# Attention scores of a two-layer step as three rounded products, with smaller buffers around them

## What is computed

```python
def _sink_attend(q, k, v, mask, sink):
    s = jnp.einsum('bqhgd,bkhd->bhgqk', q.astype(jnp.float32), k.astype(jnp.float32)) * (HEAD_DIM ** -0.5)
    if mask is not None:
        s = jnp.where(mask, s, -jnp.inf)
    sk = sink.astype(jnp.float32).reshape(1, N_KV_HEADS, GROUP, 1)
    m = jnp.maximum(jnp.max(s, axis=-1), sk)
    p = jnp.exp(s - m[..., None])
    den = jnp.sum(p, axis=-1) + jnp.exp(sk - m)
    o = jnp.einsum('bhgqk,bkhd->bqhgd', p, v.astype(jnp.float32))
    return (o / jnp.transpose(den, (0, 3, 1, 2))[..., None]).astype(q.dtype)
# latent: q = _axial_rope(q); k = _axial_rope(k); keys = [256 cached, 384 around the block of 128 queries]
# 16 heads of 64, 4 of them to each of 4 key/value heads; out = x + gate * (o * silu(g)) @ w_out
```

## Time and profile before

| | us |
|---|---|
| median of 3 runs | 2796.76 (2796.53 to 2798.9) |
| the profiled execution | 2798.01 |
| its span in the profile | 2796.2 |
| first stage (norms, loads) | about 0 to 110 |
| attention of 4 key/value heads | about 110 to 1109 |
| attention output | about 1123 to 1385 |
| mLSTM, 8 heads | about 1390 to 2590 |
| last output | to the end |

### The profile page before, as it was taken

The page is one execution under the profiler, slowest core; times in us unless marked ns, Lnnn a source line. Parts: engine busy times, 40 slices in busy tenths (PEclk is TensorE's granted clock), DMA queues, the critical chain, the costliest instruction groups (busy, mean ns, idle before and its releaser), DMA issues.

```text
span 2796.2 us, 46819 instructions
## 1 busy us (share of the span) xinstructions
PE 2690.0 (96%) x16995; PEld 2311.2 (83%) x16995; DVE 1259.6 (45%) x3434; ACT 822.2 (29%) x2140; POOL 639.2 (23%) x792
## 2 busy tenths in 40 slices
PE   6899999999999998899999999999999999998898
PEld 3687787878778786688699999899999999998787
DVE  3645637464664647555224242423334241514533
ACT  3433515242442425122213122222213131312111
POOL 2511030112113010433103031221213040303432
PEclk9999999999999999899999999999999999999999
DMA  9511030102102011344103131222222030316343
GB/s 352 204 54 55 2 96 2 54 28 69 40 17 73 24 41 68 130 136 136 41 21 82 41 69 46 60 62 36 86 36 79 18 105 16 82 41 191 109 143 106
DMA packets 183958, 213.29 MB, mean 76 GB/s; under 512 B 26288, under 2 KB 131712, under 8 KB 181840
## 3 DMA queue, kind: packets, MB, share of 16 engines
q1 hardware_dynamic: 173776, 183.18, 22.8%
q10 hardware_dynamic: 9984, 27.37, 2.5%
HBM read 172.44 MB, written 38.07 MB: 75 GB/s over the span
## 4 chain that ended last, share of the span: by engine, by line
PE 56%; DVE 2%; DMA 1%; issue 1%; POOL 0%; SPq 0%; ACT 0%; DVEq 0%; POOLq 0%
PE psum L522 11%; PE psum L524 11%; PE psum L523 11%; PE psum L1284 2%; PE psum L1285 2%; PE psum L1286 2%; PE psum L2145 2%; PE psum L1703 2%; PE psum L1705 2%; PE psum L1704 2%; PE psum L2209 2%; PE psum L2212 2%; PE psum L2193 1%; DMA m_bc<-gate_rows_mlstm 1%; PE psum L2136 1%
## 5 line engine op out<-in xcount | busy, mean ns | idle before, releaser
L522 PE MATMUL psum<-h_hi,m_w_lo 128*128 128x384 f32 (+1 forms) x1600 | 605.0, 378 | 4.7 <-DVE m_w_lo L507 3.6
L524 PE MATMUL psum<-h_hi,m_w_hi 128*128 128x384 f32 (+1 forms) x1600 | 574.4, 359 | 0.0
L523 PE MATMUL psum<-h_lo,m_w_hi 128*128 128x384 f32 (+1 forms) x1600 | 573.9, 359 | 0.0
L522 PEld LDWEIGHTS psum<-h_hi,m_w_lo 128*128 128x128 f32 x1600 | 302.0, 189 | 27.8 <-issue 5.2
L524 PEld LDWEIGHTS psum<-h_hi,m_w_hi 128*128 128x128 f32 x1600 | 301.0, 188 | 27.2
L523 PEld LDWEIGHTS psum<-h_lo,m_w_hi 128*128 128x128 f32 x1600 | 302.5, 189 | 20.4
L522 PE MATMUL psum<-h_hi,attn_w_lo 128*128 128x384 f32 (+1 forms) x800 | 291.1, 364 | 1.2 <-DVE attn_w_lo L507 0.9
L524 PE MATMUL psum<-h_hi,attn_w_hi 128*128 128x384 f32 (+1 forms) x800 | 285.8, 357 | 0.0
L523 PE MATMUL psum<-h_lo,attn_w_hi 128*128 128x384 f32 (+1 forms) x800 | 285.3, 357 | 0.0
L790 ACT ACTIVATE arena<-arena,negm 128x640 f32<-128x640 f32 (+2 forms) x208 | 161.8, 778 | 188.3 <-DVE negm L852 188.3
L491 POOL CAST m_w_hi<-m_w_raw 128x512 fp32r<-128x512 f32 x80 | 49.8, 623 | 714.5 <-PE psum L524 651.2
(11 more groups left out here) (275 smaller groups left out, 4820.1 us busy)
## 6 DMA issues: line engine op xcount, KB each, us to landing
m_bc<-gate_rows_mlstm SPq DMA_DIRECT2D x128, 256.0 KB, 3.7
m_w_raw<-in_mlstm_w_in SPq DMA_DIRECT2D x40, 512.0 KB, 4.8
h_full<-gated_output SPq DMA_DIRECT2D x31, 512.0 KB, 4.1
gated_output<-gT SPq DMA_DIRECT2D x8, 1088.0 KB, 5.1
layer_output<-xb_out ACTq DMA_DIRECT2D x17, 512.0 KB, 2.6
h_hi_full<-layer_output SPq DMA_DIRECT2D x17, 512.0 KB, 4.7
out<-h_hi_full ACTq DMA_DIRECT2D x17, 512.0 KB, 4.9
xb<-in_x_sample ACTq DMA_DIRECT2D x16, 512.0 KB, 6.4
```

The lines of the kernel that those rows point to most:

```text
L522: pe.matmul(out, self.lo[:, k, :], E.h_hi[:, k, tok], start=(k == 0), stop=False)
L523: pe.matmul(out, self.hi[:, k, :], E.h_lo[:, k, tok], start=False, stop=False)
L524: ins = pe.matmul(out, self.hi[:, k, :], E.h_hi[:, k, tok], start=False, stop=(k == KT - 1))
```

## The change

- The scores become three products of rounded parts: q_lo k_hi, q_hi k_lo, q_hi k_hi; the context block stays f32. ACT rounds keys group by group (k_hi, with the cached keys as a sixth part) and queries in four parts (q_hi); DVE makes k_lo and q_lo, which lie in the memory of kT and qT themselves. k_lo of the first two groups is made behind m=0's g=3 and g=4, of the other three behind m=1's g=0 to 2, and that of the cached keys, with q_lo, before the gate's first unit.
- ACT rounds m=1's weights before g=3 of the keys, where it did so first.
- One shuffle buffer in place of two: a shuffle waits for POOL's last addition. q_hi lies over the buffers of cosine and sine, so their first loads for m=0 and m=3 also wait until the scores are done.
- `sarg` is gone: the sink's exponential is exp(negm + sink) with the sink as bias, one instruction for each head.
- The weights' difference in a pass is made by halves, at s = 6 and s = 8.
- `wmask` has 5 blocks; block 0 reads it as two slices, side by side in a strided view. The small statistics share a buffer, and the key/value output lies in probT.
- The attention output's weights come 5 of 8 slices ahead in place of 6, by two loads.
- In the mLSTM steps the second slice `ahead(2s+1)` comes before the products of the values.

```diff
+        split = lambda name, at0, cols: nc.alloc_sbuf_tensor_at(name, [P, cols], F32R, offset=at0)
+        k_lo = split("k_lo", sb.at, KREQ)
         kT = sb("kT", [P, KCOLS])
         gT = sb("gT", [P, T])
         vS = sb("vS", [P, VTILES, HD])
+        q_lo = split("q_lo", sb.at, SAMPLE)
         qT = sb("qT", [P, T])
         spare = E.arena
+        q_hi = split("q_hi", E.arena_at + 3 * 4 * D, SAMPLE)
...
-        shuf = [spare[:, 5, b * 512:(b + 1) * 512] for b in range(2)]
-        pair = spare[:, 6:8, :].rearrange("p a n -> p (a n)")
-        prob = [pair[:, b * 640:(b + 1) * 640] for b in range(3)] + [sb("prob3", [P, 640])[:, :]]
+        shuf = spare[:, 5, 0:512]
+        flat = spare[:, :, :].rearrange("p a n -> p (a n)")
+        prob = [flat[:, 5 * D + 512 + b * 640:5 * D + 512 + (b + 1) * 640] for b in range(4)]
...
+                    if g == 0 and m != 1:
+                        sp.wait_ge(s_S, at(kv * (2 * NU) + (NU if m == 3 else 0)))
...
-                        n_ahead = E.w_ahead
-                        sp.dma_start(spare[:, 0:n_ahead, :], E.a["attn_w_out"][0].rearrange("(k p) m -> p k m", p=P)[:, 0:n_ahead, :]).then_inc(s_wo, 16)
+                        w_out = E.a["attn_w_out"][0].rearrange("(k p) m -> p k m", p=P)
+                        sp.dma_start(spare[:, 0:3, :], w_out[:, 0:3, :]).then_inc(s_wo, 16)
+                        sp.wait_ge(s_S, at(NKV * (2 * NU)))
+                        sp.dma_start(spare[:, 3:E.w_ahead, :], w_out[:, 3:E.w_ahead, :]).then_inc(s_wo, 16)
...
-                    J.act_hi(act, kv * 5 + 1, kv * 6 + 3)
                     for g in range(NG):
+                        if g == 3:
+                            J.act_hi(act, kv * 5 + 1, kv * 6 + 3)
...
+                        act.wait_ge(s_kdup, at(kv * NG + g + 1))
+                        act.copy(k_hi[:, keys_part(g)], kT[:, keys_part(g)]).then_inc(s_khi, 1)
...
-                            act.wait_ge(s_sarg, at(bbase + b + 1))
-                            act.activation(esink[:, b % 2, :], sarg[:, b % 2, :], ACT.Exp).then_inc(s_es, 1)
+                            for hh in range(2):
+                                col = kv * 4 + 2 * sub + hh
+                                ins = act.activation(esink[:, b % 2, hh:hh + 1], negm[:, b % 2, hh:hh + 1], ACT.Exp,
+                                                     bias=sink[:, col:col + 1])
+                            ins.then_inc(s_es, 1)
...
+                        act.wait_ge(s_rope, at(kv * ROPES + NG * (2 + sub)))
+                        for i in range(QPARTS):
+                            act.copy(q_hi[:, queries_part(i)], qT[:, queries_part(i)]).then_inc(s_qhi, 1)
...
-                    dve.wait_ge(s_rope, at(kv * ROPES + (rope - 1 if rope >= 2 else 0)))
+                    dve.wait_ge(s_rope, at(kv * ROPES + rope))
                     settle(E, dve)
-                    dve.stream_shuffle(shuf[b][0:rows, 0:wl], bank[0:rows, 0:wl], SWAP).then_inc(s_shuf, 1)
+                    dve.stream_shuffle(shuf[0:rows, 0:wl], bank[0:rows, 0:wl], SWAP).then_inc(s_shuf, 1)
...
-                            if hh == 1:
-                                dve.wait_ge(s_nm, at(base + w + 1))
-                                dve.wait_ge(s_es, at(bbase + (b - 1 if b >= 2 else 0)))
-                                dve.tensor_tensor(sarg[:, b % 2, :], negm[:, b % 2, :],
-                                                  sink[:, ds(kv * 4 + 2 * sub, 2)], ALU.add).then_inc(s_sarg, 1)
...
+                        def keys_low(i):
+                            c = keys_part(i)
+                            dve.wait_ge(s_khi, at(kv * (NG + 1) + i + 1))
+                            dve.tensor_tensor(k_lo[:, c], kT[:, c], k_hi[:, c], ALU.subtract).then_inc(s_klo, 1)
+
+                        def queries_low(i):
+                            c = queries_part(i)
+                            dve.wait_ge(s_qhi, at((kv * 2 + sub) * QPARTS + i + 1))
+                            dve.tensor_tensor(q_lo[:, c], qT[:, c], q_hi[:, c], ALU.subtract).then_inc(s_qlo, 1)
...
+                                if g >= 3:
+                                    keys_low(g - 3)
...
+                                if m == 1 and g < 3:
+                                    keys_low(NG - 3 + g)
                             else:
+                                if g == 0:
+                                    if m == 2:
+                                        keys_low(NG)
+                                    for i in range(QPARTS):
+                                        queries_low(i)
...
-                            if s == 6 and not (last and m == 4):
-                                J.dve_lo(dve, kv * 5 + m + 1)
+                            if s in (6, 8) and not (last and m == 4):
+                                J.dve_lo(dve, kv * 5 + m + 1, (s // 2 - 3,))
...
-                        for hh, r in enumerate(rows):
-                            pe.matmul(E.bank[2 * hh][:, 256:512], q[hh], kT[r, 0:PAST], start=True, stop=True)
-                        for hh, r in enumerate(rows):
-                            pe.matmul(E.bank[2 * hh + 1][:, 0:k1 - k0], q[hh], kT[r, k0:k1],
-                                      start=True, stop=True).then_inc(s_S, 1)
+                        t = slice(b * P, (b + 1) * P)
+                        parts = ((q_lo, k_hi), (q_hi, k_lo), (q_hi, k_hi))
+                        for n, (x, y) in enumerate(parts):
+                            for hh, r in enumerate(rows):
+                                pe.matmul(E.bank[2 * hh][:, 256:512], x[r, t], y[r, 0:PAST], start=(n == 0), stop=(n == 2))
+                        for n, (x, y) in enumerate(parts):
+                            for hh, r in enumerate(rows):
+                                ins = pe.matmul(E.bank[2 * hh + 1][:, 0:k1 - k0], x[r, t], y[r, k0:k1],
+                                                start=(n == 0), stop=(n == 2))
+                                if n == 2:
+                                    ins.then_inc(s_S, 1)
...
-                    pe.wait_ge(s_rope, at(kv * ROPES + NG * (2 + sub)))
+                    pe.wait_ge(s_qlo, at((kv * 2 + sub) * QPARTS + QPARTS))
                     pe.wait_ge(s_release, at(kv * NB + NG * m))
                     if sub == 0:
                         pe.wait_ge(s_kdup, at(kv * NG + NG))
-                        pe.wait_ge(s_ckl, at(kv * 16 + 16))
+                        pe.wait_ge(s_klo, at(kv * (NG + 1) + NG + 1))
...
+                        ahead(2 * s + 1)
...
-                        ahead(2 * s + 1)
...
-    window = np.concatenate([own, own, prev, own, nxt] + [own, own, own, nxt], 1)
+    window = np.concatenate([own, own, prev, own, nxt], 1)
```

More of the change, by code:

```diff
@@ L570, in phase_attn @@
         s_wo = sem("w_out_loaded")
+        s_khi, s_klo, s_qhi, s_qlo = (sem(x) for x in ("keys_hi", "keys_lo", "queries_hi", "queries_lo"))
         (s_shuf, s_cos, s_rope, s_gth, s_release, s_kdup, s_vT, s_vS, s_kvo, s_kvst, s_ckl, s_cvl,
@@ L608, in scores_of, with window, keys_part @@
             return pair[:, first:first + width(w // 2)]
+        def window(b):
+            if b == 0:
+                return bass.AP(tensor=E.wmask[:, :].tensor, offset=0, ap=[[MASK, P], [3 * P, 2], [1, 2 * P]])
+            return E.wmask[:, 0:width(b)]
+        def keys_part(i):
+            if i == NG:
+                return slice(0, PAST)
+            t0, wl, wc = lat_ctx(i)
+            return slice(KLAT + t0, KLAT + t0 + wl)
+        queries_part = lambda i: slice(i * 512, i * 512 + 512)
+        QPARTS = SAMPLE // 512
         weighted, spread = E.bank[6][:, 0:P], E.bank[6][:, P:2 * P]
@@ L763, in _ @@
                     act.copy(kvout[:, 1, :], E.bank[6][:, 0:HD]).then_inc(s_kvo, 1)
+                    act.wait_ge(s_ckl, at(kv * 16 + 16))
+                    act.copy(k_hi[:, keys_part(NG)], kT[:, keys_part(NG)]).then_inc(s_khi, 1)
                     for sub in range(2):
@@ L844, in softmax_max @@
                             n = width(b)
-                            m0 = WFIRST if b == 0 else WMID
                             dve.wait_ge(s_S, at(base + w + 1))
@@ L849, in softmax_max @@
                             dve.wait_ge(s_p, at(base + (2 * b - 2 if b >= 2 else 0)))
-                            dve.wait_ge(s_sarg, at(bbase + (b - 1 if b >= 2 else 0)))
+                            dve.wait_ge(s_es, at(bbase + (b - 1 if b >= 2 else 0)))
                             settle(E, dve)
-                            dve.tensor_tensor_reduce(prob[w % 4][:, 0:n], scores_of(w), E.wmask[:, m0:m0 + n],
+                            x, y = prob[w % 4][:, 0:n], scores_of(w)
+                            if b == 0:
+                                x, y = (t.rearrange("p (a n) -> p a n", a=2) for t in (x, y))
+                            dve.tensor_tensor_reduce(x, y, window(b),
                                                      scale=-(HD ** -0.5), scalar=nsk[:, 2 * sub + hh:2 * sub + hh + 1],
```

(4 more changed lines are left out.)

37 lines of the change are left out of this document (18 added, 19 removed).

## The result

The changed kernel takes **2812.1 us** (median of 5, 2810.31 to 2814.23) beside 2796.76 us (2795.03 to 2800.23) before: 15.3 us more, a ratio of 1.0052, interval 1.0038 to 1.0067. The forecast was 2791, with a range that ended at 2801. It is slower by more than the 0.2% that can be told from no change, the outcome that had been given 0.12. The profiled execution has a span of 2812.4 us and a mean granted clock of 0.985.

The account below looks back on a forecast made before the run. Two equal attention bounds, PE's work and the DVE/ACT chain. Passes -9.6, key heads +9.6, mLSTM -4.8 and loads -0.7 sum to -5.5 us: 2792.5 on the profiled 2798.0, 2791.3 against the median; forecast 2791, range 2780 to 2801.

Parts of the forecast that it names:

- What bounds the kernel: Attention steps: PE's own work, 3.88 us a step, and the chain through DVE and ACT, 3.875, bind equally.
- The score parts: Attention scores: three rounded products shorten a block's score time S by 0.19 us; blocks 0 and 1 give -0.33 a pass.
- exposed loads: Rival in the attention scores: weight loads of each part are not hidden, +28 us, 2829 in all; 7%.
- unpaired heads: Rival in the attention scores: heads' pairs not side by side in rounded form, parts three times as long, near 2870; 3%.
- the sink's exponential: Attention chain on ACT: a second instruction ahead of the copies adds 0.094 us, leaving 3.825 us a step.
- -9.6 us for the passes: Attention, eight passes: shorter scores less the second sink exponential give -1.2 us a pass, 0 to -15 in all.
- The key head: Start of the three key heads after the first: rotary rounds in series and the keys' difference add 3.2 us each, +9.6.
- The clock: Rival at the key heads: the 3.2 us stalls make the granted clock fall, +5 us, 2796; 10%.
- ACT's cast: Key head: the weights' cast, moved behind k's third group, is ready at about 385.6, so it isn't last.
- The split of the weights' difference: Attention steps 6 and 8: two halves of 0.64 us on DVE instead of one 1.28, worth 0.
- mLSTM: mLSTM heads: projection matmuls fill 0.68 us of each of seven PE waits for m_bc, -4.8 us (0 to -6.7).
- The mask: Loads: the mask loses 262 KB where queues are full, -0.7 us, or 0 if another load decides.

Follow-up runs that it names:

- e4_sink_one: The changed kernel with the sink's exponential again one plain instruction on a sum made by DVE; 2797.8 us, ratio 0.9988 to the kernel before.
- e12_two_plain: The changed kernel with DVE's sum back and the sink's exponential as two one-column instructions without bias; 2802.1 us, ratio 1.0006 to the kernel before.
- e6_sink_late: The changed kernel with the two biased sink exponentials behind ACT's copies and DVE's denominators behind its own copy; 2784.3 us, ratio 0.9943 to the kernel before.
- e10_before_late: The kernel before, f32 scores, with its one plain sink exponential behind the copies and the denominators late; 2794.4 us, ratio 0.9988.
- e7_best: The changed kernel with second shuffle buffer, keys' difference behind the weights', ACT's weights cast first, and late sink exponentials; 2765.1 us, ratio 0.9884 to the kernel before.
- e2_keys_low_later: The changed kernel with the first difference of the keys behind the weights' difference, one shuffle buffer; 2804.3 us, ratio 1.0012 to the kernel before.
- e9_filler: The changed kernel with 30 identity transposes on PE during the wait for the weights' difference at key heads 1 to 3; 2803.9 us, ratio 1.0022 to the kernel before.

## Why the prediction was wrong, point by point

- **What bounds the kernel.** Right: two equal bounds, the lap of two steps made of the chain and of PE's 2.58. In the changed kernel the chain is 5.24 (scores at 308.30, turn of the same block at 313.54), which gives (5.24 + 2.58)/2 = 3.91 where 3.905 was measured. That is little more than adding up, since one step is the chain's length and the next follows from it. The proof is in what the rule said before each run: a mean of 3.77 for e4_sink_one, 3.765 measured; a long step of 3.95 for e12_two_plain, 3.95 measured; a mean of 3.73 for e6_sink_late, 3.72 measured; 3.87 unmoved for e10_before_late, 3.87 measured.
- **The score parts.** Right. 0.12 and 0.17 us apart, S 0.23 shorter where 0.19 was counted, and blocks 0 and 1 gained 0.36 us a pass (starts 5.27 and 6.34 apart, from 5.44 and 6.53) where 0.33 was. The rivals of exposed loads and unpaired heads fell. The rule of the Trainium skill (TensorE: Matmul & The Clock Gate, The mechanism), that loads overlap running matmuls only in other rows, isn't borne out here either: the load of the next part of the same rows, 0.19 us, would not fit between starts 0.12 apart.
- **The sum failed at the sink's exponential.** "A small one there holds it 0.09 us" was read from a plain instruction, and the new ones have a bias. The chain gained about 0.2 and lost 0.28, not 0.094, and -9.6 us for the passes became +0.4 and +0.5 between them: 10.5 us of the 21.7 by which the span was missed. This is the step that failed: the price of the second exponential was taken as 0.09 us more on the chain, and it was 0.28, of which e12_two_plain puts 0.09 to the second instruction and 0.18 to the two biases. I gave this price one value where the trace of before had no such row (a small instruction with a bias), and 0 as the worst of the passes, where a loss was possible too. The Trainium skill (ScalarE: Activation LUTs, What ACT_TABLE_LOAD costs) has the price: each operand of one value per partition adds about 93 ns to an ACTIVATE. The runs agree, with 0.185 against 0.094 us from one to the next. With 0.09 the estimate of 3.825 was good: two plain exponentials measured 3.81, and 8.5 us less over the passes where 9.6 was forecast.
- **The key head.** The mechanism of the wait was right, and the second step that failed is that the clock behind it was left out of the sum. The waits grew by 11.3 us (12.2 in four from 0.9 in three) where 9.6 were forecast, the three long ones 3.9 to 4.0 each; 1.2 us of the excess is the first half of the weights' difference, 1.48 us in each of the three heads for about 1.08 before, and why it was longer no run shows. The clock, held as a rival at 10% and at 5 us, came in each of the three heads and cost about 6.5. The pause of 3.6 us with a fall behind it stood in the earlier trace rows, and the forecast of 3.2 for the new pause was near enough that it belonged into the main case. ACT's cast, "so it isn't last", was the next in line: 0.87 us when the others were out of the way.
- **The split of the weights' difference**, 0. Borne out in the changed kernel: 4.04, 3.77 and 4.40 are 0.73 us above three steady steps (3.67, 4.14, 3.67), and the kernel before has 0.75 above. It is worth about 0.5 us a pass in the best version, where ACT's exponentials are off the chain.
- **mLSTM.** Right: seven waits of 0.27 us, 4.8 us less waiting, 5.6 by the distance of the heads.
- **The mask.** 0.7 was counted, nothing is seen in the two executions profiled: DVE starts its first shuffle of the keys, the end of the first stage's chain, at 118.85 us before and at 118.82 with the change. That the first pass starts 1.5 later goes with a fall of the clock for 3.4 us in the first stage of that execution, and the other profiled runs with the same mask have more or fewer such falls (first starts at 173.8 to 180.3 us); so it is no term of the change.
- **Sum.** Forecast -5.5 on the span, measured +16.2: passes and what is between them 10.5 more, key heads 8.4 more, the start 2.2 more, the rest 0.6 more.

## What to carry to other kernels

When two bounds are equal, price the edit on both: here PE's saving was paid back on ACT by two instructions that stood on the chain, and moving them behind the copies that PE waits for, with DVE's denominators behind its own copy, was worth 25 us in the passes. When a buffer is merged to make room, ask which rounds ran at once because of it, and look for memory that is idle in that phase (a probability buffer served). A pause of PE is to be priced with a possible fall of the clock behind it: in these key heads pauses of 2.3 us and less had none, those of 2.6 and 2.7 one each, those of 3.6 and more all had one. The length of one pause does not decide it alone: in the first stage pauses of 2.65 us (e7_best, at 100.1) and 2.66 (e2_keys_low_later, at 103.0) had no fall behind them, and one of 1.89 (e12_two_plain, at 92.5) had one of 3.4 us.

## What the runs showed of the hardware

- Of two exponentials of one column in a row, each holds ACT 0.185 us with a bias operand (changed kernel) and 0.094 without (e12_two_plain).
- Rounded 32-bit products of 64 rows run in pairs, 0.12 us a part at 256 columns and 0.173 at 384, with the weights of every part changed.
- The granted clock fell to 0.50 for 3.4 or 6.8 us behind pauses of 3.9 to 4.0 us, in each of the three key heads of the changed kernel that had them, and stayed at 1.00 when transposes filled all but 0.6 to 0.8 us of the same time (e9_filler).
